# Seven block products in place of eight for four of eleven pairs of weight tiles in two down projections

## The chip, the core and the metric

The kernel runs on one core of a Trainium2 chip. The time is that of the device, in microseconds (us), of one execution; the median of several is given. TensorE (PE in the profile) multiplies, with its weight loads shown as PEld; VectorE is DVE, ScalarE is ACT, GpSimd is POOL, and the queue of weight loads is that of SyncE (SP).

## The reference

The program is one layer of each of three kinds on 256 rows of 1024 numbers in float32: a block with two feed-forward networks (FFN) around gMLP gating and stick-breaking attention, a gated linear attention with an FFN, and a block attention with an FFN. The change touches only the FFNs of the last two, each of which is followed by a layer norm:

```
def swiglu_ffn(x, w_gu, w_down):
    gate, up = jnp.split(x @ w_gu, 2, axis=-1)
    return (jax.nn.silu(gate) * up) @ w_down
```

with x of 256 x 1024, `w_down` of 2816 x 1024, and then `x = layer_norm(ALPHA * x + ffn(x))`, where ALPHA is the fourth root of 4.

## The kernel before

All products are made in three matmuls of "fp32r" type: each factor is split into a high part and a low part, and high x high, high x low and low x high are added in PSUM. Weights come in chunks of 128 x 1024 numbers (two k-tiles of 512 columns, in the down projection). A chunk goes four ways, each on another engine. SyncE's queue loads it into one of 5 slots of `raw` (`load_chunk`; the slot is free when the chunk 5 before it has been split, semaphore `wl`). ScalarE copies it, rounded, into `wh` (`high_to`, line 1000). VectorE subtracts that from `raw` into `wl` (`low_to`, line 1594); both have 9 slots. TensorE uses both and counts the chunk in `used`, which frees the slots. `lead` says how many chunks ahead of TensorE the two converting engines stand in their program order; each engine's order is written out by hand, as generators (`block`) that yield at each chunk.

An FFN has a gate and an up product in column blocks (`narrow`: nine of 256 columns, turned, so that their results already have the hidden dimension on partitions), whose product goes through HB and is split into HH and HL; and then the down projection, blocks `d0` and `d1`, one for each half of 512 output columns. Each has 22 k-tiles in 11 chunks. For each chunk TensorE makes, for both row tiles t (128 rows each), 2 k-tiles x 3 matmuls = 6 matmuls of 512 columns, so 12 in all (`pe_products`, lines 514, 521, 529). The last 5 chunks of `d1` are run first for t = 0 and then for t = 1 (`tail`), so that the layer norm of the first row tile can begin while the second is still multiplied.

VectorE adds the result of each half and row tile to `ALPHA * X` (`residual`, line 1703), takes the statistics and norms X in two passes (`layer_norm`, lines 1683 to 1698), first with `gbc`, then with `bbc`; between the two it needs the inverse root `rs`, which GpSimd computes from the variance (line 2440). `gbc` and `bbc`, the norm's gain and shift, are loaded by GpSimd's queue when the previous stage is done. In the third FFN TensorE then turns X's pieces (line 439), for the next stage: those of the first row tile before the last k-tile of the down projection, those of the second row tile in the last chunk of the next block's first row tile. In the fourth X is stored.

## Time and profile before

| what | us |
|---|---|
| median of 3 runs | 1223.21 |
| lowest and highest of them | 1222.98, 1224.38 |
| span of the profiled execution | 1221.8 |

Of one profiled execution there is a page, with busy times, the chain of work that ended last, and the costliest groups of instructions, and there are the rows of single instructions. A row gives the start, the duration, engine and line, what is written from what, and in brackets the idle time of that engine before it with what ended it. Matmuls overlap, and the end of each is a model: what one costs is read from the distance of two starts.

### The profile page before, as it was taken

The page shows a single profiled execution, that of the slowest core. Times are in us where ns is not written, and L with a number is a line of the kernel's source. Part 1 is how long each engine was busy: PE and PEld are TensorE (multiplying, and loading weights), DVE is VectorE, ACT ScalarE, POOL GpSimd, SP SyncE. Part 2 cuts the span into 40 slices and gives each one's busy share as a digit, 9 for nine tenths or more (in the row PEclk, how much of TensorE's full clock was granted, in tenths as well). Part 3 has the DMA queues.
Part 4 walks back from the last instruction along what each step waited for, and adds up shares of the span by engine and source line. Part 5 has one row for each costly group of instructions (what it writes and reads, how often), then busy time and mean ns, then how long its engine had stood idle before and what let it go on. Part 6 is the DMA issues. An engine that isn't in the chain of part 4 may idle for free.

```text
span 1221.8 us, 15988 instructions
## 1 busy us (share of the span) xinstructions
PE 1211.0 (99%) x6145; PEld 1019.5 (83%) x6145; DVE 827.1 (68%) x1190; ACT 647.3 (53%) x923; POOL 41.5 (3%) x85
## 2 busy tenths in 40 slices
PE   9999999999999999999999999999999999999997
PEld 7888888888787888888888888888888888888886
DVE  5987755756676666777547677667647777667753
ACT  7565644446666355556436554556534464556640
POOL 2000002100000000000010000000000000000000
PEclk9999999999999999999999999999999999999999
DMA  8676754754545556666647556566745444766551
GB/s 281 197 210 187 245 186 136 248 176 145 154 141 170 188 174 208 193 187 194 202 141 189 189 189 221 176 190 190 258 173 170 158 139 140 239 190 189 190 195 46
DMA packets 154747, 225.81 MB, mean 185 GB/s; under 512 B 8152, under 2 KB 85984, under 8 KB 154672
## 3 DMA queue, kind: packets, MB, share of 16 engines
q1 hardware_dynamic: 152144, 216.10, 55.7%
q0 software_dynamic: 2512, 8.69, 2.6%
q8 instruction: 49, 0.80, 0.3%
q14 instruction: 26, 0.21, 0.1%
q10 hardware_dynamic: 16, 0.00, 0.0%
HBM read 223.72 MB, written 1.05 MB: 184 GB/s over the span
## 4 chain that ended last, share of the span: by engine, by line
PE 96%; DMA 1%; DVE 1%; ACT 1%; issue 0%; SPq 0%; POOL 0%; DVEq 0%; ACTq 0%; POOLq 0%
PE ps L550 23%; PE ps L514 19%; PE ps L521 18%; PE ps L529 18%; PE ps L554 12%; PE ps L439 2%; DMA wgk<-in_gla_w_gk_dram 1%; PE ps L713 1%; PE ps L726 1%; DMA raw<-in_ff_w_gate_dram 0%; ACT wh L1000 0%; PE ps L929 0%; PE ps L696 0%; PE ps L899 0%; PE ps L655 0%
## 5 line engine op out<-in xcount | busy, mean ns | idle before, releaser
L1594 DVE TENSOR_TENSOR wl<-raw,wh 128x1024 fp32r<-128x1024 f32 x405 | 486.3, 1219 | 104.6 <-ACT wh L1000 101.8
L1000 ACT ACTIVATE wh<-raw 128x1024 fp32r<-128x1024 f32 x405 | 418.4, 1051 | 100.8 <-PE ps L529 42.1
L550 PE MATMUL ps<-XT,wh 128*128 128x512 f32 x1216 | 423.0, 392 | 0.0
L554 PE MATMUL ps<-XT,wl 128*128 128x256 f32 x1216 | 339.7, 279 | 0.0
L550 PEld LDWEIGHTS ps<-XT,wh 128*128 128x128 f32 x1216 | 227.6, 187 | 50.9
L554 PEld LDWEIGHTS ps<-XT,wl 128*128 128x128 f32 x1216 | 229.5, 189 | 0.2
L514 PE MATMUL ps<-wh,XT 128*128 128x512 f32 x510 | 203.3, 399 | 0.0
L521 PE MATMUL ps<-wl,XT 128*128 128x512 f32 x510 | 199.4, 391 | 0.2 <-DVE wl L2372 0.2
L529 PE MATMUL ps<-wh,XT 128*128 128x512 f32 x510 | 157.9, 391 | 0.0
L514 PE MATMUL ps<-wh,HHf 128*128 128x512 f32 x352 | 137.3, 390 | 0.0
L521 PE MATMUL ps<-wl,HHf 128*128 128x512 f32 x352 | 137.0, 389 | 0.0
L514 PEld LDWEIGHTS ps<-wh,XT 128*128 128x128 f32 x510 | 95.8, 188 | 21.0 <-issue 0.7
L521 PEld LDWEIGHTS ps<-wl,XT 128*128 128x128 f32 x510 | 95.9, 188 | 20.1 <-DVE wl L2372 1.3
L529 PEld LDWEIGHTS ps<-wh,XT 128*128 128x128 f32 x510 | 95.2, 188 | 19.8
L529 PE MATMUL ps<-wh,HLf 128*128 128x512 f32 x352 | 108.5, 389 | 0.0
L529 PEld LDWEIGHTS ps<-wh,HLf 128*128 128x128 f32 x352 | 66.1, 188 | 13.9
L514 PEld LDWEIGHTS ps<-wh,HHf 128*128 128x128 f32 x352 | 66.1, 188 | 13.6
L521 PEld LDWEIGHTS ps<-wl,HHf 128*128 128x128 f32 x352 | 66.1, 188 | 13.4
L1113 ACT ACTIVATE HBf<-ps 128x256 f32<-128x256 f32 x72 | 27.5, 385 | 71.9 <-PE ps L554 71.9
L1113 ACT ACTIVATE SGf<-ps 128x256 f32<-128x256 f32 x72 | 27.6, 385 | 61.3 <-PE ps L554 61.3
L1719 DVE TENSOR_TENSOR HBf<-ps,HBf 128x256 f32<-128x256 f32 x72 | 30.3, 424 | 42.0 <-ACT HBf L1113 40.3
L1719 DVE TENSOR_TENSOR SGf<-ps,SGf 128x256 f32<-128x256 f32 x72 | 30.1, 423 | 27.9 <-ACT SGf L1113 27.9
(296 smaller groups left out, 1039.9 us busy)
## 6 DMA issues: line engine op xcount, KB each, us to landing
raw<-in_ffn_w_gu_dram SPq DMA_DIRECT2D x88, 512.0 KB, 4.3
raw<-in_w_in_dram SPq DMA_DIRECT2D x56, 512.0 KB, 4.1
raw<-in_ff_w_up_dram SPq DMA_DIRECT2D x44, 512.0 KB, 4.6
raw<-in_ff_w_down_dram SPq DMA_DIRECT2D x44, 512.0 KB, 4.6
raw<-in_ffn_w_down_dram SPq DMA_DIRECT2D x44, 512.0 KB, 4.6
raw<-in_ff_w_gate_dram SPq DMA_DIRECT2D x40, 512.0 KB, 4.1
raw<-in_gla_w_in_dram SPq DMA_DIRECT2D x24, 512.0 KB, 4.6
raw<-in_moba_w_in_dram SPq DMA_DIRECT2D x24, 512.0 KB, 4.8
```

Of the source, the lines that this page charges most:

```text
L439: ins = e.transpose(ps[:, aux_bank(key), i * P:(i + 1) * P], src, ident[:, :])
L514: e.matmul(o, lh[:, kt, rows(t)], high[:, w], start=kt == 0, stop=False)
L521: e.matmul(o, lh[:, kt, rows(t)], low[:, w], start=False, stop=False)
L529: ins = e.matmul(o, ll[:, kt, rows(t)], high[:, w], start=False, stop=kt == kts - 1)
L550: e.matmul(o, wh_of(j)[:, w], XT[:, kt, :, :].rearrange("p a n -> p (a n)"), start=kt == 0, stop=False)
L554: ins = e.matmul(o[:, 0:256], wl_of(j)[:, w], XTH[:, kt, :], start=False, stop=kt == kts - 1)
L713: ins = e.matmul(o, QK[r, m, keys], QK[r, m, queries], start=True, stop=True)
L726: ins = e.matmul(y, V[:, t, 64 * h:64 * h + 64], z, start=t == 0, stop=t == 1)
L1000: e.activation(wh_of(j)[:, 0:m], raw[:, j % NR, 0:m], ACT.Copy).then_inc(S("wh"), 1)
L1113: e.activation(dst, ps[:, bank_of(name, t), 256:512], ACT.Copy).then_inc(S("part"), 1)
L1594: e.tensor_tensor(wl_of(j)[:, 0:m], raw[:, j % NR, 0:m], wh_of(j)[:, 0:m].bitcast(F32), ALU.subtract).then_inc(S("wl"), 1)
L1719: e.tensor_tensor(dst, ps[:, bank_of(name, t), 0:256], dst, ALU.add).then_inc(ev(name, t)[0], 1)
```

## The change

Take one pair of k-tiles k and k+1. Its share of the output is a product of a 2 x 2 block matrix (two row tiles by two k-tiles, of h) with another (two k-tiles by two column halves, of the weights). That takes eight block products. For four of the eleven pairs in each of the two FFNs, those of the hidden blocks `SEVEN = (1, 2, 3, 7)`, seven products of sums and differences are made in their place.

- **Sums of h.** VectorE makes four sums of 128 columns in a chain (`row_sums`), ScalarE and VectorE split them into SH and SL (`high_sums`, `low_sums`). The fourth set is split into XT at the start of the down projection.
- **Sums of the weights.** A pair has two loads, of one k-tile with all 1024 columns each, and makes four chunks: block 1 of the first tile (512 columns), the second tile, and two chunks of sums. GpSimd makes these (`weight_sums`): one difference over 1024 columns (`wsum`), then two operations over 512 columns in a chain (`wchain`). They go into SC for the first and third pair, into `gbc` and `bbc` for the second and fourth. A slot of `raw` is free when the chunk has been split and GpSimd has read it.
- **Products.** `pe_seven` makes 21 matmuls in place of 24. Three of the seven products go to PSUM banks of the block's outputs, four to banks 7, 6, 5 and 4, added up over the four pairs.
- **Putting it together.** ScalarE scales X by ALPHA during the down projection. After the last such pair, and behind the chunk conversions that `d0` has brought ahead, ScalarE copies the four banks to SBUF (`take`). GpSimd adds them to each other and to X in eight operations over 512 columns (`gather`), in front of the two inverse roots of the layer norm. VectorE adds the ordinary outputs to X. The addition for half 0 and row tile 1 now comes between the norm of the first row tile and the addition for half 1 and row tile 1.
- **Order.** The chunks of both halves are mixed in `d0` (25 chunks): two pairs with both halves, then four times four chunks of a seven-product pair and an ordinary one of half 0, then one more; `d1` keeps five. `gbc` and `bbc` are loaded for the norm when the last sum has been split.

```diff
+SEVEN_FFNS = ("f3", "f4")
+SEVEN = (1, 2, 3, 7)
...
+            def seven(s):
+                k = 2 * (SEVEN[s] + 2)
+                mixed[f].append(("seven", s, len(chunks)))
+                for kt, n in ((k, 1), (k + 1, 2)):
+                    chunks.append((wd[kt * P:(kt + 1) * P, :].rearrange("p (k n) -> p k n", k=2), n, 512, kt))
+                for _ in range(2):
+                    chunks.append((None, 2, 512, k))
...
+            products = [[(of_h(k, top), p1, first, last)],
+                        [(of_h(k + 1, top), upper[0], False, False), (of_sums(3), upper[1], False, False)],
+                        [(of_sums(0), p5, first, last), (of_sums(2), p7, first, last)],
+                        [(of_sums(1), p6, first, last), (of_h(k + 1, bottom), lower, False, False)]]
...
+                    s1, s2, s3, s4 = [SG[:, i % 2, rows(r)] for r in range(4)]
+                    own(e.tensor_tensor(s1, a21, a22, ALU.add))
+                    e.tensor_tensor(s3, a11, a21, ALU.subtract)
+                    wait_own()
+                    own(e.tensor_tensor(s2, s1, a11, ALU.subtract))
+                    wait_own()
+                    e.tensor_tensor(s4, a12, s2, ALU.subtract).then_inc(S("ssum"), 1)
...
+                        e.tensor_tensor(t13.rearrange("p (a n) -> p a n", a=2), raw[:, a:a + 2, cols(1)],
+                                        raw[:, a, :].rearrange("p (a n) -> p a n", a=2),
+                                        ALU.subtract).then_inc(S("wsum"), 1)
...
+                    own(e.tensor_tensor(t24[:, cols(0)], t13[:, cols(1)], raw[:, a, cols(0)], ALU.add))
+                    e.tensor_tensor(t24[:, cols(1)], raw[:, b, cols(0)], t24[:, cols(0)], ALU.subtract).then_inc(
+                        S("wchain"), 1)
...
+                if f in SEVEN_FFNS:
+                    kind, s, j = [item for item in mixed[f] if item[0] == "seven"][-1]
+                    e.wait_ge(S("used"), j + 4)
+                    e.wait_ge(S("hl"), len(NARROW) * (FFNS.index(f) + 1))
+                    for i, dst in enumerate((SG[:, 0, :], SG[:, 1, :], HB[:, 3, :], HB[:, 2, :])):
+                        take(i, dst)
...
+                    if f in SEVEN_FFNS:
+                        e.wait_ge(S("gathered"), 4 * SEVEN_FFNS.index(f) + 2 * t + half + 1)
+                        o = product_of(name, t)
+                        e.tensor_tensor(X[:, t, cols(half)], o, X[:, t, cols(half)], ALU.add).then_inc(
+                            ev(name, t)[0], 1)
+                        layer_norm(name, t, half, 6 if f == "f3" else 8)
...
+                e.wait_ge(S("alpha"), 2 * F + 2)
+                e.wait_ge(S("taken"), 4 * F + 2)
+                own(add(p6, p1))
+                add(X[:, 0, cols(0)], p1).then_inc(S("gathered"), 1)
+                own(add(X[:, 0, cols(1)], p6))
+                e.wait_ge(S("taken"), 4 * F + 3)
+                add(X[:, 0, cols(1)], p5).then_inc(S("gathered"), 1)
+                e.wait_ge(S("taken"), 4 * F + 4)
+                own(add(p7, p6))
+                add(X[:, 1, cols(0)], p7).then_inc(S("gathered"), 1)
+                own(add(X[:, 1, cols(1)], p7))
+                add(X[:, 1, cols(1)], p5).then_inc(S("gathered"), 1)
```

VectorE at the end of the fourth FFN's last up block and the start of its down projection, before (HLf is h's low part, wl a chunk's):

```order
L1719 TENSOR_TENSOR HBf<-ps,HBf 128x256 [waits s_part] x2
L1760 TENSOR_TENSOR HBf<-HBf,SGf 128x512 [waits s_silu,s_ev1,s_ev0]
L1594 TENSOR_TENSOR wl<-raw,wh 128x1024 [waits s_wh,s_hsum]
L1724 TENSOR_TENSOR HLf<-HBf,HHf 128x512 [waits s_hh]
L1594 TENSOR_TENSOR wl<-raw,wh 128x1024 [waits s_wh] x10
L1703 SCALAR_TENSOR_TENSOR X<-X,ps 128x512 [waits s_mm0]
```

The same place after:

```order
L1882 TENSOR_TENSOR HBf<-ps,HBf 128x256 [waits s_part] x2
L1942 TENSOR_TENSOR HBf<-HBf,SGf 128x512 [waits s_silu,s_ev1,s_ev0]
L1757 TENSOR_TENSOR wl<-raw,wh 128x512 [waits s_wh,s_hsum]
L1757 TENSOR_TENSOR wl<-raw,wh 128x1024 [waits s_wh]
L1757 TENSOR_TENSOR wl<-SC,wh 128x1024 [waits s_wh] x2
L1887 TENSOR_TENSOR HLf<-HBf,HHf 128x512 [waits s_hh]
L1904 TENSOR_TENSOR XT<-SGf,XT 128x512 [waits s_sh]
L1757 TENSOR_TENSOR wl<-raw,wh 128x1024 [waits s_wh]
L1757 TENSOR_TENSOR wl<-raw,wh 128x512 [waits s_wh]
L1757 TENSOR_TENSOR wl<-raw,wh 128x1024 [waits s_wh]
L1757 TENSOR_TENSOR wl<-gbc,wh 128x1024 [waits s_wh]
L1757 TENSOR_TENSOR wl<-bbc,wh 128x1024 [waits s_wh]
```

The splits of sums stand in the same row as those of loaded chunks, one split of h's sums has come in, and the addition to X has gone to the far side of all of them.

GpSimd in the fourth FFN, before (the roots of the previous norm, the loads, the roots of the last norm):

```order
L2440 TENSOR_TENSOR st<-st 128x1 [waits s_agg]
L2440 TENSOR_TENSOR st<-st 128x1 [waits s_agg,s_rs0]
L2421 DMA gbc<-in_ln_g_dram 128x1024 [waits s_xg11,s_rs1]
L2424 DMA bbc<-in_ln_b_dram 128x1024
L2440 TENSOR_TENSOR st<-st 128x1 [waits s_agg]
L2440 TENSOR_TENSOR st<-st 128x1 [waits s_agg,s_rs0]
```

And after, from the sums of the fourth pair on:

```order
L2652 TENSOR_TENSOR gbc<-raw 128x1024 [waits s_raw1,s_raw0,s_wl]
L2660 TENSOR_TENSOR bbc<-gbc,raw 128x512 [waits s_wsum]
L2661 TENSOR_TENSOR bbc<-raw,bbc 128x512 [waits s_pl]
L2616 DMA gbc<-in_ln_g_dram 128x1024 [waits s_wl]
L2619 DMA bbc<-in_ln_b_dram 128x1024
L2672 TENSOR_TENSOR SGf<-SGf 128x512 [waits s_taken,s_alpha]
L2672 TENSOR_TENSOR X<-X,SGf 128x512 [waits s_pl]
L2672 TENSOR_TENSOR X<-X,SGf 128x512
L2672 TENSOR_TENSOR X<-X,HBf 128x512 [waits s_taken,s_pl]
L2672 TENSOR_TENSOR HBf<-HBf,SGf 128x512 [waits s_taken]
L2672 TENSOR_TENSOR X<-X,HBf 128x512 [waits s_pl]
L2672 TENSOR_TENSOR X<-X,HBf 128x512
```

The sums and the additions stand in front of the roots, and the two loads have moved behind the last sum.

ScalarE at the end of the fourth FFN, before (conversions of the last chunks):

```order
L1000 ACTIVATE wh<-raw 128x1024 [waits s_raw4,s_used]
L1000 ACTIVATE wh<-raw 128x1024 [waits s_raw0,s_used]
L1000 ACTIVATE wh<-raw 128x1024 [waits s_raw1,s_used]
L1000 ACTIVATE wh<-raw 128x1024 [waits s_raw2,s_used]
L1000 ACTIVATE wh<-raw 128x1024 [waits s_raw3,s_used]
```

And after, with the copies out of PSUM (L1268):

```order
L1138 ACTIVATE wh<-raw 128x1024 [waits s_raw1,s_used]
L1138 ACTIVATE wh<-raw 128x1024 [waits s_raw2,s_used]
L1138 ACTIVATE wh<-raw 128x1024 [waits s_raw3,s_used]
L1268 ACTIVATE SGf<-ps 128x512 [waits s_hl,s_used]
L1268 ACTIVATE SGf<-ps 128x512
L1268 ACTIVATE HBf<-ps 128x512 x2
```

The four copies stand behind the last conversion; in the third FFN they stand behind that of the next stage's second chunk.

## Rows read from the trace of the kernel before

**Rows 1.** The page's chain that ended last, by engine.

```profile
PE 96%; DMA 1%; DVE 1%; ACT 1%; issue 0%; SPq 0%; POOL 0%; DVEq 0%; ACTq 0%; POOLq 0%
```

**Rows 2.** Busy time by stretch, both down projections: length, PE, PEld, DVE, ACT, POOL, PEclk.

```profile
862.95:922.80 59.85, 59.85 (x271) 49.62 (x269) 34.86 (x37) 24.05 (x25) 0.99 (x1) 1.00 0.57 194
1154.56:1214.45 59.89, 59.89 (x266) 49.37 (x264) 30.05 (x33) 19.56 (x20) 1.00 (x1) 1.00 0.38 133
```

**Rows 3.** Timeline of TensorE in the fourth down projection, six matmuls apart.

```profile
1165.48 0.39 PE L514 MATMUL ps<-wh,HHf 128*128 128x512 f32 x1
...
1166.84 0.39 PE L514 MATMUL ps<-wh,HHf 128*128 128x512 f32 x1
```

**Rows 4.** Groups by form: line, engine, operation, count, busy us, mean ns.

```profile
L1594 DVE TENSOR_TENSOR wl<-raw,wh 128x1024 fp32r<-128x1024 f32 x404 | 486.0, 1221 | 104.6 <-ACT wh L1000 101.8
L1000 ACT ACTIVATE wh<-raw 128x1024 fp32r<-128x1024 f32 x404 | 418.1, 1053 | 100.8 <-PE ps L529 42.1 <-DMA raw<-in_ffn_w_down_dram 21.0 <-DMA raw<-in_ff_w_down_dram 10.3
...
L1724 DVE TENSOR_TENSOR HLf<-HBf,HHf 128x512 fp32r<-128x512 f32 x36 | 24.6, 684 | 0.0
...
L1251 ACT ACTIVATE QK<-ps 128x512 f32<-128x512 f32 x8 | 4.7, 592 | 2.9 <-PE ps L439 2.9
```

**Rows 5.** Timeline of VectorE in the fourth down projection; brackets: idle before.

```profile
1158.17 5.76 DVE L1594 TENSOR_TENSOR wl<-raw,wh 128x1024 fp32r<-128x1024 f32 x5
...
1183.36 0.69 DVE L1703 SCALAR_TENSOR_TENSOR X<-X,ps 128x512 f32<-128x512 f32 x1 [9.92 <-PE ps L529]
```

**Rows 6.** Timeline of VectorE over one step of the gate and up loop.

```profile
1144.60 0.69 DVE L1760 TENSOR_TENSOR HBf<-HBf,SGf 128x512 f32<-128x512 f32 x1
...
1149.63 0.42 DVE L1719 TENSOR_TENSOR SGf<-ps,SGf 128x256 f32<-128x256 f32 x1 [0.96 <-ACT SGf L1113]
1150.58 1.23 DVE L1594 TENSOR_TENSOR wl<-raw,wh 128x1024 fp32r<-128x1024 f32 x1 [0.52 <-ACT wh L1000]
...
1153.85 0.42 DVE L1719 TENSOR_TENSOR HBf<-ps,HBf 128x256 f32<-128x256 f32 x1 [0.58 <-ACT HBf L1113]
1155.18 0.42 DVE L1719 TENSOR_TENSOR HBf<-ps,HBf 128x256 f32<-128x256 f32 x1 [0.90 <-ACT HBf L1113]
1155.69 0.69 DVE L1760 TENSOR_TENSOR HBf<-HBf,SGf 128x512 f32<-128x512 f32 x1
```

**Rows 7.** Timeline of GpSimd, two memsets.

```profile
1.74 0.20 POOL L2409 MEMSET ones<- 128x128 f32 x1
...
665.57 0.74 POOL L2507 MEMSET STm<- 128x768 f32 x1 [24.24 <-DVE KT L2225]
```

**Rows 8.** Timelines of GpSimd, and of VectorE beside it at 202.58.

```profile
197.11 0.18 POOL L2427 TENSOR_SCALAR st<-st 128x1 f32<-128x1 f32 x1
...
202.64 1.22 POOL L2427 TENSOR_SCALAR LNB<-LNB 128x2 f32<-128x2 f32 x1 [0.55 <-DVE LNB L1901]
...
202.58 1.23 DVE L1594 TENSOR_TENSOR wl<-raw,wh 128x1024 fp32r<-128x1024 f32 x1
...
628.36 0.56 POOL L2497 TENSOR_TENSOR st<-st 128x1 f32<-128x1 f32 x1 [174.68 <-DVE st L1673]
...
1209.78 1.00 POOL L2440 TENSOR_TENSOR st<-st 128x1 f32<-128x1 f32 x1 [171.70 <-DVE st L1689]
```

**Rows 9.** Timelines of VectorE and ScalarE: splits, and the conversion that waits for the reload.

```profile
1186.06 7.08 DVE L1594 TENSOR_TENSOR wl<-raw,wh 128x1024 fp32r<-128x1024 f32 x6
...
1190.81 1.06 ACT L1000 ACTIVATE wh<-raw 128x1024 fp32r<-128x1024 f32 x1 [5.03 <-DMA raw<-in_ffn_w_down_dram]
```

**Rows 10.** Timelines at the ends of the third (VectorE, TensorE) and fourth FFN (TensorE, VectorE).

```profile
927.70 1.42 DVE L1698 SCALAR_TENSOR_TENSOR X<-X,st,bbc 128x512 f32<-128x512 f32 x2
...
928.75 1.08 PE L439 MATMUL ps<-ident,X 128*128 128x128 f32 x8
...
1213.99 0.61 PE L529 MATMUL ps<-wh,HLf 128*128 128x512 f32 x2
...
1214.64 0.69 DVE L1703 SCALAR_TENSOR_TENSOR X<-X,ps 128x512 f32<-128x512 f32 x1 [2.08 <-PE ps L529]
```

210 lines of the change are left out of this document (188 added, 22 removed).

## Prediction, made before the changed kernel was run

> **What bounds the kernel now.** I read the page first: TensorE carries 96% of the chain that ended last [rows 1]. The stretches of the two down projections come next: in each TensorE is busy for every microsecond, at full granted clock [rows 2]. One chunk of twelve matmuls takes 1.36 us per six, so one matmul of 512 columns costs 0.227 us [rows 3]. Here, then, a matmul taken away is time taken away, as long as nothing else becomes late. What feeds TensorE is the pair of conversions of each weight chunk: 1.05 us on ScalarE, 1.22 us on VectorE (1.15 us apart in a row) [rows 4, 5]. VectorE is free for 9.9 us in the middle of the down projection [rows 5], so it has room today.
>
> **The saving.** A pair of k-tiles took 8 block products of 3 matmuls and takes 7: 3 matmuls fewer for each of 4 pairs in 2 FFNs, 24 x 0.227 = **5.44 us**, 2.72 us per FFN. By this alone the profiled span would go from 1221.8 to 1216.4 us.
>
> I count time in one FFN from the start of its down projection (1154.56 us in the fourth, 862.95 in the third), and number its chunks c0 to c29 (normal c0 to c3; then four times: four chunks of a seven-product pair and a normal one; c24; and c25 to c29, the last five of half 1). Of a seven-product pair the first chunk is 512 wide, the third and fourth are sums. Without a stall TensorE needs c8 at 15.6, c17 at 29.2, c22 at 36.7, c25 at 43.5, and is done with row tile 0 at 50.3 and with all at 57.1 us (before: 53.0 and 59.8).
>
> **Added work in the gate and up loops.** Per seven-product block: four VectorE operations of 128 columns in a chain with two waits (0.68 us for 512 columns and 1.22 for 1024 [rows 4] make 0.28 for 128, with the waits 1.3 us), one split of 512 columns (0.68 us), and one copy of 0.6 us on ScalarE. One step of that loop lasts 11.09 us and VectorE idles in it for 3.0 us, in waits that TensorE paces [rows 6]; 2.0 us fit in, with 1 us over. I cost it at nothing. If the cover were short, a step would start late by what is missing, but product banks have slack: the gate product is out at 1150.05 [rows 6], and its banks are needed at 1154.6.
>
> **Added work on VectorE and ScalarE in the down projection.** Four pairs turn 2 chunks of 1024 into 3.5: 6 chunks more, 6 x 1.15 = 6.9 us on VectorE and 6.3 on ScalarE. Beside 9.9 us of idle VectorE this is hidden. The two scalings of X (1.05 us each) and four copies out of PSUM (0.6 us [rows 4]) on ScalarE replace nothing but lie in idle time as well.
>
> **The weight sums on GpSimd.** Per pair one operation over 1024 columns and two over 512 that form a chain, each reading two operands. No row has such an operation. Bounds: not under VectorE's price for the same (1.2 us for 1024 [rows 4]); from above, three streams (two reads, a write) at the slope of GpSimd's memset, (0.74 - 0.20) / 640 columns = 0.84 ns a column [rows 7], 2.6 us. One read through memset's rate takes 0.9 us, so two reads alone give 1.7. I take 2.2 us for 1024 and 1.1 for 512, between two and three streams: 4.4 us per pair. The Trainium skill (GPSIMD Engine Reference, section 3, Performance versus the Vector engine) gives about 2.6 cycles an element for a two-input add, 4497 ns for 2048 columns; an estimate by it would be 2.3 us for 1024, the same sum within 0.2 us a pair, and no run here shows it yet.
>
> **The collision.** On GpSimd an operation on two elements takes 0.18 us alone, but 1.22 us when it starts 0.06 us after VectorE's 1.23 us split of a chunk, which reads two SBUF tiles; the root of one element takes 0.56 us alone, 1.00 in the fourth FFN's layer norm, where VectorE works on X and gbc [rows 8]. GpSimd is held until such an operation of VectorE is over. I take it that this works both ways: then the sums and the splits, which all read two SBUF tiles, go one after the other. That VectorE is held by GpSimd no row shows, as GpSimd never had a long operation. The Trainium skill (SBUF — State Buffer, section on the two separate sides) states it: the port pair is an exclusive lock, whoever starts first has it for the whole instruction. By that rule the sums come out as in my forecast, without it as in rival B; with the rows on GpSimd's side it agrees.
>
> The two then take turns. Work on that port from -0.5 us until c22 is split: VectorE 4 x 0.62 + 15 x 1.15 for c4 to c22, 1.2 for c3, 2.0 for the last product of h and two splits, together 22.9; GpSimd 2.2 for what is left of the first pair and 3 x 4.4 = 15.4. Sum 38.3, so c22 is ready at 37.8 at best where 36.7 is needed. The order makes it worse earlier: c8 is split at about 15, and the slot of raw that it frees holds c15 about 4.5 us later (3.6 in [rows 9], where one load stands alone), so the third pair's sums can't start before 20, their chain ends at about 26, c16 is split by 27.5, the fourth pair's first sum takes the port for 2.2 us, and c17 is split at 31 against 29.2, c18 0.8 us late on top. I take **2.0 us** of stall per FFN (0 to 5).
>
> **The tail.** ScalarE's four copies stand behind the conversion of c29 (of the next stage's second chunk, c31, in the third FFN), not behind the last seven-product pair alone. By the same turns c22 is split at 38.3 and c24 at 40.6; the load into its slot lands 3.6 us later [rows 9], conversion until 45.3, second copy at 46.5. Then GpSimd does eight additions of 1.1 us with 0.1 between, 9.6 us, and 2.2 us of waits for VectorE's splits and X operations: 58.3. Behind them on GpSimd stand the roots of both layer norms, 0.56 to 1.0 us; behind the first root VectorE has its last two X operations (1.4) and the moved residual of half 0 (0.7 + 0.7): free at 61.9. TensorE's last product would be there at 57.1 + 2.0, and is taken some 0.25 us later [rows 10], at 59.4: **2.5 us** late in the fourth FFN (0 where the copies come at 40). In the third all is 2.7 us later (two more chunks to load and convert, one more split in the way): X's first half is normed at 63.2 where TensorE turns it at 56.2 + 2.0, 5.0 us; and the moved residual (1.4 us) and the split behind it meet the split of the turned X, which today ends just in time (X is ready at 929.1, TensorE turns it from 928.75 [rows 10]): 1.0 us more, **6.0 us**. The reloads of gbc and bbc are issued behind the last sum, at about 35, and land by 41, long ahead of 52.
>
> **Sum.** -5.4 + 2 x 2.0 + 2.5 + 6.0 = +7.1 us: a span of 1228.9. The profiled run of 1221.8 lies 1.4 us under the median, so 1230.3; I say **1230.0**. I hold the ends of the unknown costs to -5 and +14.
>
> **Rivals.** A, the forecast: the port is shared by turns both ways. Range 1226 to 1236.
> B: VectorE isn't held by GpSimd's reads, or GpSimd gives way. Then splits run as today: c24 at 30, copies from 38, additions until 51, the roots in time. What stays is about 0.4 us for the moved residual in the third FFN: -5.0, 1218.2. For it speaks that no row shows VectorE held (in [rows 8] it keeps its durations); against it, that GpSimd plainly waits for VectorE on the same port.
> C: shared port but shorter sums, 1.7 us for 1024: the port's work falls by 3.5 us per FFN, the first stall vanishes, the tail shrinks to 1 us and 3: -1.4, 1221.8, inside what can't be told from no change or just outside.
> D: as A, and the stalls of 4 to 6 us let the granted clock fall to 1.2 GHz at the head of the next stage. No wait that long stands in the middle of this trace [rows 2], so nothing here prices it but the ratio of the levels: 5 us of matmuls at half speed cost 5 more: 1235 to 1242.
> E: the seven products aren't paced at 0.227 us, since each matmul has weights of its own. But each has them already in [rows 3]: little chance.
>
> **How the numbers follow.** A 0.48, B 0.27, C 0.15, D 0.07, others 0.03. About 0.2% (2.4 us) is what a measurement of this kernel tells from no change. Faster: B and a third of C, 0.33. Within: half of C and bits of A, 0.11. Slower: 0.56. The range that leaves out no more than 2 in 10 must take B in: 1217.5 to 1237. The likeliest case alone is 1226 to 1236.
>
> **What would show it.** GpSimd's subtraction over 1024 columns with a start-to-start near 2.2 us or more; splits beside it that last 2 to 3.5 us, or begin that much late, where they take 1.22 alone. TensorE waiting for wl in front of c17 and c18 of either FFN. The additions on X ending around 58, and the root behind them; X's second operation waiting for GpSimd. If splits keep 1.22 us beside the sums and the chain stays 96% TensorE, B is right and I am wrong by 12 us. If the third FFN's end shows no wait for the turned X, the tail's term fails even if the first stall is there.

## The result, and the profile after

The changed kernel takes 1238.34 us (median of 4 runs, 1237.21 to 1238.52) against 1223.45 for the kernel before: 1.0115 times as long (95% interval 1.0101 to 1.013). That is 14.9 us slower by the medians and 14.1 by the ratio. I had said 1230.0, within 1217.5 to 1237. The direction was right and the size was not: the sum said +7.1 us, the spans of the two profiled executions differ by 14.7 (1236.5 against 1221.8). One execution among all of those below, the profiled one of e13, was slow from end to end (2032.49 us, granted clock 0.556), so its time is left out and its rows aren't used.

Three anchors tell where the time lies: the third FFN's down projection starts at 862.67 us (862.95 before), the fourth's at 1165.01 (1154.56), and the last instruction ends at 1236.5 (1221.8). So 10.7 us were lost from the third down projection to the fourth, 4.2 in the fourth and behind it, and nothing ahead of either. TensorE's waits come first. Timeline of TensorE in the changed kernel, third FFN and then fourth; brackets are the idle time and what ended it:

```profile
893.22 0.50 PE L660 MATMUL ps<-wl,SHf 128*128 128x512 f32 x1 [0.89 <-DVE wl L1757]
...
895.46 0.50 PE L602 MATMUL ps<-wl,HHf 128*128 128x512 f32 x1 [0.58 <-DVE wl L1757]
...
929.60 1.97 PE L520 MATMUL ps<-ident,X 128*128 128x128 f32 x8 [8.44 <-DVE X L1861]
931.22 0.77 PE L595 MATMUL ps<-wh,HHf 128*128 128x512 f32 x1
...
939.23 1.03 PE L520 MATMUL ps<-ident,X 128*128 128x128 f32 x8
...
1193.84 0.50 PE L660 MATMUL ps<-wl,SHf 128*128 128x512 f32 x1 [0.53 <-DVE wl L1757]
...
1196.08 0.50 PE L660 MATMUL ps<-wl,SHf 128*128 128x512 f32 x1 [0.58 <-DVE wl L1757]
...
1198.31 0.50 PE L602 MATMUL ps<-wl,HHf 128*128 128x512 f32 x1 [0.58 <-DVE wl L1757]
```

There are two kinds of wait. At c17, the last chunk of the third seven-product pair, and at c18 behind it TensorE waits for low parts, in the fourth FFN at c16 as well: counted from start to start, less the 0.23 us of a matmul, 1.8 us in the third FFN and 2.2 in the fourth. (The first matmul behind each such wait takes 0.34 us to the next start, 0.11 more than the others.) And in the third FFN it waits 8.44 us for the first row tile of the turned X. The transposes behind that wait take 1.97 us where they took 1.04, and from them to the transposes of row tile 1 pass 9.63 us where 6.82 passed before (921.93 to 928.75, the latter in [rows 10]). These 2.8 us show in the granted clock, and in the starts: the matmuls of 512 columns from 931.22 to 934.35 us start 0.43 us or more apart, those from 935.57 on 0.23. Busy time by stretch (length, PE, PEld, DVE, ACT, POOL, PEclk, DMA share, GB/s):

```profile
902.00:912.00 10.00, 10.00 (x46) 8.29 (x45) 5.40 (x5) 3.57 (x4) 0.00 (x0) 1.00 0.89 330
...
922.00:932.00 10.00, 2.40 (x10) 2.30 (x11) 8.19 (x12) 0.99 (x2) 6.60 (x5) 0.66 0.18 52
932.00:942.00 10.00, 10.00 (x41) 7.98 (x41) 7.68 (x14) 4.68 (x7) 2.05 (x3) 0.83 0.31 97
```

TensorE worked without a pause, stood for 8.4 us, and came back at the lower of its two levels, 1.2 and 2.4 GHz; 0.66 and 0.83 of full speed are the means of ten microseconds each. The transposes at 1.97 us are at the lower level, those at 939.23, at 1.03 us, at the full one again.

What comes late is read off the three other engines. GpSimd, third FFN: a pair of weight sums, then the loads of the norm, then the additions and the root.

```profile
889.68 2.40 POOL L2652 TENSOR_TENSOR gbc<-raw 128x1024 f32<-128x1024 f32 x1
892.16 2.16 POOL L2660 TENSOR_TENSOR bbc<-gbc,raw 128x512 f32<-128x512 f32 x1
894.40 2.15 POOL L2661 TENSOR_TENSOR bbc<-raw,bbc 128x512 f32<-128x512 f32 x1
900.80 0.59 POOL L2616 DMA_DIRECT2D gbc<-in_ln_g_dram  x1 [4.25 <-DVE wl L1757]
...
916.06 1.30 POOL L2672 TENSOR_TENSOR SGf<-SGf 128x512 f32<-128x512 f32 x1 [14.14 <-ACT SGf L1268]
...
923.64 4.59 POOL L2672 TENSOR_TENSOR X<-X,HBf 128x512 f32<-128x512 f32 x3
928.20 0.56 POOL L2635 TENSOR_TENSOR st<-st 128x1 f32<-128x1 f32 x1
```

ScalarE beside it: the conversions of chunks c27 and c28, and the copies out of PSUM.

```profile
903.02 1.06 ACT L1138 ACTIVATE wh<-raw 128x1024 fp32r<-128x1024 f32 x1 [0.21 <-DMA raw<-in_ffn_w_down_dram]
909.41 1.06 ACT L1138 ACTIVATE wh<-raw 128x1024 fp32r<-128x1024 f32 x1 [5.33 <-DMA raw<-in_ffn_w_down_dram]
...
914.85 1.06 ACT L1268 ACTIVATE SGf<-ps 128x512 f32<-128x512 f32 x2
```

VectorE: the split of c17 and three more beside sums of GpSimd, then the norm of row tile 0.

```profile
890.91 2.26 DVE L1757 TENSOR_TENSOR wl<-SC,wh 128x1024 fp32r<-128x1024 f32 x1 [2.33 <-ACT wh L1138]
893.09 5.14 DVE L1757 TENSOR_TENSOR wl<-raw,wh 128x1024 fp32r<-128x1024 f32 x3
...
918.76 0.69 DVE L1975 TENSOR_TENSOR X<-ps,X 128x512 f32<-128x512 f32 x1 [2.56 <-POOL X L2672]
...
924.11 3.00 DVE L1855 SCALAR_TENSOR_TENSOR X<-X,st,gbc 128x512 f32<-128x512 f32 x2
928.79 1.42 DVE L1861 SCALAR_TENSOR_TENSOR X<-X,st,bbc 128x512 f32<-128x512 f32 x2 [1.68 <-POOL st L2635]
```

The split of c17 lasts 2.26 us, from 890.91 on, beside the fourth pair's first sum (889.68 to 892.08), and three splits in a row take 5.14 us where five took 5.76 in [rows 5]. L1855 takes 3.00 us for two; with no GpSimd beside it, it takes 1.40 to 1.41. The operation at 918.76 has GpSimd's additions beside it too and keeps its 0.69 us: one of its operands is in PSUM and only one in SBUF, where the held ones read two SBUF tiles. The turned X waits for L1861, that for the root, the root for the eight additions, these for the copies, the copies for the conversions of c28 to c31, and c28 for its load.

The fourth FFN ends by the same chain, without a turned X behind it. VectorE there:

```profile
1226.70 1.41 DVE L1861 SCALAR_TENSOR_TENSOR X<-X,st,bbc 128x512 f32<-128x512 f32 x2 [1.68 <-POOL st L2635]
...
1229.36 0.67 DVE L1975 TENSOR_TENSOR X<-ps,X 128x512 f32<-128x512 f32 x1
...
1232.65 1.42 DVE L1861 SCALAR_TENSOR_TENSOR X<-X,st,bbc 128x512 f32<-128x512 f32 x2
```

TensorE's last product is out at 1224.9, and VectorE takes it at 1229.36. From 1224.9 to the end pass 11.6 us, where 7.2 passed before (1214.6 to 1221.8): a tail of 4.4 us.

### The profile page after: what moved, and what is told of

Its sections match the earlier page's. It is cut to its first block and busy times, and to the rows that moved or that the text cites. A ratio compares the mean times of both kernels' runs of the same rounds, so it can differ in the third digit from the quotient of the medians.

```text
span 1236.5 us, 16140 instructions
## 1 busy us (share of the span) xinstructions
PE 1209.7 (98%) x6121; PEld 1016.0 (82%) x6121; DVE 882.0 (71%) x1246; ACT 670.6 (54%) x959; POOL 121.0 (10%) x127
## 5 line engine op out<-in xcount | busy, mean ns | idle before, releaser
L1757 DVE TENSOR_TENSOR wl<-raw,wh 128x1024 fp32r<-128x1024 f32 x405 | 495.8, 1243 | 102.5 <-ACT wh L1138 99.9
L1138 ACT ACTIVATE wh<-raw 128x1024 fp32r<-128x1024 f32 x405 | 413.9, 1042 | 83.6 <-PE ps L610 21.7
L602 PE MATMUL ps<-wl,HHf 128*128 128x512 f32 x288 | 112.6, 391 | 1.2 <-DVE wl L1757 1.2
L595 PE MATMUL ps<-wh,HHf 128*128 128x512 f32 x288 | 112.8, 392 | 0.0
L610 PE MATMUL ps<-wh,HLf 128*128 128x512 f32 x288 | 89.2, 391 | 0.0
L602 PEld LDWEIGHTS ps<-wl,HHf 128*128 128x128 f32 x288 | 54.2, 188 | 12.9 <-DVE wl L1757 2.0
L610 PEld LDWEIGHTS ps<-wh,HLf 128*128 128x128 f32 x288 | 54.3, 189 | 11.5
L595 PEld LDWEIGHTS ps<-wh,HHf 128*128 128x128 f32 x288 | 54.2, 188 | 11.1
L1175 ACT ACTIVATE XT<-ps 128x512 fp32r<-128x512 f32 x24 | 13.5, 597 | 60.7 <-PE ps L520 60.7
```

The lines of the kernel that those rows point to most:

```text
L595: e.matmul(o, lh[:, kt, rows(t)], high[:, w], start=kt == 0, stop=False)
L602: e.matmul(o, lh[:, kt, rows(t)], low[:, w], start=False, stop=False)
L610: ins = e.matmul(o, ll[:, kt, rows(t)], high[:, w], start=False, stop=kt == kts - 1)
L1138: e.activation(wh_of(j)[:, 0:m], source(j), ACT.Copy).then_inc(S("wh"), 1)
L1175: e.activation(dst, src, ACT.Copy).then_inc(high(key)[0], 1)
L1757: e.tensor_tensor(wl_of(j)[:, 0:m], source(j), wh_of(j)[:, 0:m].bitcast(F32), ALU.subtract).then_inc(S("wl"), 1)
```

## The experiments

Theory at the start: the two engines share a port of the SBUF and are held by each other, which costs the chunks' stalls; what was mis-sized is the tail, since c28 came late and with it the copies and additions. Rivals: VectorE is not held; the root is what holds; VectorE would be too full anyway. Each ratio below is to the kernel before on the same chip, with its 95% interval. That kernel's median was 1224.35 us beside e1 to e4, 1223.26 beside e5 to e8, 1223.19 beside e9 to e12 and 1224.91 beside e13 to e15; so where two kernels are compared, it is by what each stands above or below the kernel before measured beside it (the changed one 14.9 above).

**e1: the port alone.** The kernel before, with five operations of GpSimd over 1024 columns at the start of each of the two down projections:

```diff
+                    for _ in range(5):
+                        if stage == 6:
+                            own(e.memset(low, 0.0))
+                        else:
+                            own(e.tensor_tensor(low, low, high, ALU.subtract))
```

> The kernel before, with five operations of GpSimd over 128x1024 put into its idle time, beside VectorE's row of splits at the head of a down projection: in the third FFN memsets, which read nothing from SBUF; in the fourth differences of two SBUF tiles. They write a tile that nothing reads afterwards, so the output is whole. Theory (VectorE and GpSimd take turns where both read SBUF tiles): in the fourth FFN splits beside a difference last up to 3.5 us in place of 1.22 and start late, each difference takes 2.2 us alone and up to 3.4 beside a split; in the third FFN splits stay 1.15 us apart. Rival 1 (GpSimd gives way, VectorE isn't held): splits stay 1.15 us apart in both. Rival 2 (any operation of GpSimd slows VectorE): they stretch in both. The time moves by under 1 us in all cases, since splits are well ahead.

One execution, 1223.21 us, where the kernel before had 1222.81 to 1225.51. Timelines of GpSimd's memsets and of a split beside them (third FFN), then of GpSimd's differences and VectorE beside them (fourth):

```profile
861.52 5.00 POOL L2526 MEMSET SC<- 128x1024 f32 x5 [115.26 <-DVE wl L1594]
...
864.61 1.23 DVE L1594 TENSOR_TENSOR wl<-raw,wh 128x1024 fp32r<-128x1024 f32 x1
...
1153.08 14.79 POOL L2528 TENSOR_TENSOR SC<-SC 128x1024 f32<-128x1024 f32 x5 [115.27 <-DVE wl L1594]
...
1156.14 3.32 DVE L1594 TENSOR_TENSOR wl<-raw,wh 128x1024 fp32r<-128x1024 f32 x1
1159.38 2.89 DVE L1724 TENSOR_TENSOR HLf<-HBf,HHf 128x512 fp32r<-128x512 f32 x1
```

Beside differences a split takes 3.32 us in place of 1.23 and a half split 2.89 in place of 0.69: VectorE is held for 2.1 to 2.2 us, nearly a whole operation of GpSimd. It isn't beside memsets: they run from 861.52 to 866.52 us, and the split that falls among them keeps its 1.23 us. This rests on that split and two operations of 512 columns (0.69 us each, at 863.88 and 865.75), since the memsets were over when VectorE's row of splits began at 866.36. The Trainium skill (SBUF — State Buffer, section on the two separate sides) calls this port an exclusive lock; this trace agrees, in the direction that no row of before showed. Rival B has fallen.

**e2, e3, e4: sums, additions, and both, cut to one column.** Every instruction and wait stays, and nearly all of the work goes. In e2:

```diff
-                    if b == a + 1:
-                        e.tensor_tensor(t13.rearrange("p (a n) -> p a n", a=2), raw[:, a:a + 2, cols(1)],
-                                        raw[:, a, :].rearrange("p (a n) -> p a n", a=2),
-                                        ALU.subtract).then_inc(S("wsum"), 1)
...
+                    e.tensor_tensor(t13[:, 0:1], raw[:, a, 512:513], raw[:, b, 0:1], ALU.subtract).then_inc(S("wsum"), 1)
...
```

> The changed kernel with the weight sums made over one column in place of 1024 and 512, all waits kept; the weight sums are thereby left out of the computation. Theory: without long operations of GpSimd the splits run 1.15 us apart, no matmul waits for wl in either FFN (-4 us), chunks c24 to c31 are ready earlier, so the four copies come at about 40 us of the down projection in place of 52, and the eight additions are over before the roots (-14 us of tails): 1218 to 1221 us. Rival (the order of chunks, the added splits and the added waits are themselves what is late): over 1230 us still.

Measured: 1220.7 us, 0.9971 (0.996 to 0.9983), as the theory said. TensorE waits for no low part in the down projections; for the turned X it waits 1.9 us. The copies come at 43.5 us of the down projection (905.69), not quite at 40.

In e3, and with both edits in e4:

```diff
-                return e.tensor_tensor(dst, dst, src, ALU.add)
+                return e.tensor_tensor(dst[:, 0:1], dst[:, 0:1], src[:, 0:1], ALU.add)
```

> The changed kernel with the eight additions of GpSimd over one column in place of 512; most of the sum of the seven products is thereby left out. Theory: the wait for splits at c17 to c22 stays (2 us per FFN), both tails go, since the roots have nothing long in front of them: 1221 to 1224 us. Rival (tails come from late copies alone, whatever GpSimd then does): above 1230 us.

Measured: 1227.27 us, 1.0026 (1.0016 to 1.0035), 3 us over the expected band. The chunks' stalls stayed, 1.8 us in the third FFN and 1.2 in the fourth. What I had missed: without any real addition the copies still come at 915.7 us, VectorE's first operation on X waits for them, and TensorE waits 2.0 us for the turned X and then takes 8.61 us to the next turn, not 6.82.

> The changed kernel with both, the weight sums and the eight additions, over one column. Theory: all that the 24 matmuls give is there: 5.4 us less, 0.4 us given back by the moved addition in the third FFN: 1218 to 1219 us. Rival (the added work of VectorE and ScalarE, or the matmuls of other weights, cost something themselves): 1221 us or more.

Measured: 1218.27 us, 0.9951 (0.9936 to 0.9967). By the medians 6.1 us are gone, by the interval 4.0 to 7.8, which holds the 5.4. The trace is sharper. TensorE's two turns in the third FFN:

```profile
920.12 1.04 PE L520 MATMUL ps<-ident,X 128*128 128x128 f32 x8
...
926.94 1.27 PE L520 MATMUL ps<-ident,X 128*128 128x128 f32 x8
```

The down projection starts at 863.86 here, so the turns come 56.26 and 63.08 us into it, against 58.98 and 65.80 before: 2.72 us less, as forecast. From the start of the fourth (1154.74) to the end (1219.3) pass 64.56 us against 67.24, 2.68 less. So the saving is there in both, and the row sums of h, their splits, the extra chunks and copies cost nothing to be seen in them. (The span of this one execution is only 2.5 us shorter, as it started the third FFN 0.9 us later and took 2.0 us more from the second turn to the fourth down projection; why stays open.)

The parts don't add up. Taking the additions away gives 12.0 us, taking the sums away gives 18.5, both give 21.0. The sums are the larger part, and the additions cost mostly in their wake: 12.0 us with the sums in place, 2.4 without them (e2 against e4).

**e5: the norm's loads out of the weight loads' way.**

```diff
+                if stage in (6, 8):
+                    e.wait_ge(S("taken"), 4 * SEVEN_FFNS.index(f) + 1)
                 load_g(ln_g[i, k].partition_broadcast(P))
                 load_b(ln_b[i, k].partition_broadcast(P))
```

> The changed kernel, but GpSimd issues the two loads of the norm's gamma and beta tiles only after the first of the four PSUM copies (the wait stands in front of each of the two norm stages of the third and the fourth FFN), so that they no longer share the DMA engines with the weight chunks c26 to c29. Theory (the copies come about 4 us later than forecast, because ScalarE's conversions of c28 to c31, which stand ahead of the copies, wait for chunks whose loads are slowed by the norm's loads): the chunk behind ScalarE's longest DMA wait lands 2 to 4 us sooner, the copies come 2 to 4 us sooner, TensorE's wait for the turned X shrinks from 8.4 us to 5 or 6, and the time is 1232 to 1236 us. Rival (the load was late because its slot was freed late by the weight sums; the norm's loads did not matter): the same copies, within 1 us, and 1237 to 1239 us.

Measured: 1234.34 us, 1.0086 (1.0071 to 1.0101), in the theory's band. The wait for the turned X is 6.94 us, where the theory had 5 or 6. ScalarE of e5, the conversion of c28 and the copies:

```profile
906.33 1.06 ACT L1138 ACTIVATE wh<-raw 128x1024 fp32r<-128x1024 f32 x1 [2.56 <-DMA raw<-in_ffn_w_down_dram]
...
911.69 1.07 ACT L1268 ACTIVATE SGf<-ps 128x512 f32<-128x512 f32 x2
```

Two loads of 512 KB that I had costed at nothing delay c28 and the copies by 3.1 us on the trace's axis, by 2.5 counted from the start of the down projection (862.10 here, 862.67 in the changed kernel), and the end by 3.8. From the split that frees its slot to its conversion c28 takes 5.3 us here and 7.8 in the changed kernel. GpSimd's first addition comes only 2.1 us sooner (913.97 against 916.06), since the two loads now stand in front of it.

**e6: the copies ahead of the conversion of c28.**

```diff
+                        if j == seventh + 9:
...
+                            e.wait_ge(S("used"), seventh + 4)
+                            e.wait_ge(S("hl"), len(NARROW) * (FFNS.index(f) + 1))
+                            for i, dst in enumerate((SG[:, 0, :], SG[:, 1, :], HB[:, 3, :], HB[:, 2, :])):
+                                e.activation(dst, ps[:, SEVEN_BANKS[i], :], ACT.Copy).then_inc(S("taken"), 1)
...
                     e.wait_ge(*source_ready(j))
                     e.activation(wh_of(j)[:, 0:m], source(j), ACT.Copy).then_inc(S("wh"), 1)
```

> The changed kernel with ScalarE's four PSUM copies placed ahead of its conversion of the fourth weight chunk from the end, right behind the last seven-product chunk that TensorE has used, in place of behind all conversions. Theory (the late copies are the mis-sized term): the copies come some 10 us sooner, GpSimd's eight adds begin and end as much sooner and no longer hold up the sums of the norm in the third FFN; there TensorE's wait for the turned X falls under 3 us and the clock stays up; the stalls of 2 us per FFN at the seven-product chunks stay: 1227 to 1231 us. Rival (the eight adds collide with VectorE's last conversions instead and move the wait into the chunks of half 1): TensorE waits for the low parts of the last chunks, 3 to 6 us per FFN in place of the tail, and the time is 1233 to 1238 us.

Measured: 1229.43 us, 1.0048 (1.0033 to 1.0063), in the theory's band. It gives 8.7 us for moving four copies. But TensorE still waits 3.55 us for the turned X, where the theory said under 3, and loses 1.9 us by the clock behind it. VectorE of e6:

```profile
911.30 8.81 DVE L1759 TENSOR_TENSOR wl<-raw,wh 128x1024 fp32r<-128x1024 f32 x4 [5.34 <-ACT wh L1146]
920.04 0.68 DVE L1977 TENSOR_TENSOR X<-ps,X 128x512 f32<-128x512 f32 x1
```

The early additions run beside the last splits: four take 8.81 us, where they take 5.09 in e9. So in part the rival's collision happened too: TensorE waits for low parts at 913.48 and 915.71, 1.8 us from start to start, and the rest lands in the wait for the turned X.

**e7: the root of row tile 0 between the fourth and the fifth addition.**

```diff
                 add(X[:, 0, cols(1)], p5).then_inc(S("gathered"), 1)
+                root(stage, 0)
                 e.wait_ge(S("taken"), 4 * F + 4)
...
```

> The changed kernel with GpSimd's root of row tile 0 placed between its fourth and its fifth add in the third and fourth FFN, in place of behind all eight. Row tile 0 has all of its columns after the fourth add. Theory (the root of tile 0 waits behind the adds of tile 1, and TensorE waits for that root): TensorE's wait for the turned X in the third FFN falls from 8.4 us to 3 to 5 us, the granted clock there stays above 0.9, which gives back up to 2.8 us more; in the fourth FFN little: 1230 to 1234 us. Rival (the clock falls after the shorter wait as well, or tile 1 becomes the late one): 1234 to 1237 us.

Measured: 1237.27 us, 1.0111 (1.0094 to 1.0128): a miss, 3 us above the theory's band and at the upper end of the rival's. Timelines of GpSimd and of VectorE in e7:

```profile
925.59 1.00 POOL L2634 TENSOR_TENSOR st<-st 128x1 f32<-128x1 f32 x1 [2.92 <-DVE st L1852]
...
926.96 3.21 DVE L1861 SCALAR_TENSOR_TENSOR X<-X,st,bbc 128x512 f32<-128x512 f32 x2
```

The root comes 2.6 us sooner (925.59 against 928.20). But GpSimd now idles 2.9 us for the statistics, and the additions of tile 1, pushed back, hold L1861 (3.21 us for two, 1.42 alone). The wait falls to 6.19 + 0.56 us, a new wait of 0.7 us for a low part comes in at 913.47, and the next turn of TensorE starts at 939.08, against 939.23. The time is 0.9 us lower, and the two intervals overlap. Moving the root alone trades one hold for another; this doesn't show that its place costs nothing once the additions are out of the way.

**e8: everything on VectorE**, sums ahead of the split of each pair's first chunk, additions ahead of its first operation on X, copies early.

```diff
+                    if j in group_of and group_of[j][1] == 0:
+                        sums_of_weights(j)
                     e.wait_ge(S("wh"), j + 1)
...
                 if f in SEVEN_FFNS:
+                    gather(f)
                     down(0, 0)
```

> The seven-product scheme whole, nothing of it on GpSimd: the weight sums are made on VectorE, in front of its split of the first chunk of each seven-product pair, the eight adds on VectorE in front of its last add of the down projection's half 1 for row tile 0, and ScalarE's four copies stand early. VectorE's added work is 4 pairs by about 3.7 us per FFN (1.24 us per 1024 columns of a two-input operation, 0.7 per 512) and eight adds of about 0.7 us, beside splits that no longer wait for the other engine. Theory (the price of the change is the sharing of the SBUF port between the two engines and where the adds stand, not the amount of work): the stalls at the seven-product chunks vanish or stay under 1 us per FFN and the tails come back to those of the kernel before plus at most 1 us: 1218 to 1221 us, faster than both. Rival (VectorE is too full for it: 71 per cent of the span, more in the down projection): TensorE waits for low parts by 3 us or more per FFN, 1224 to 1230 us.

Measured: 1226.34 us, 1.0027 (1.0017 to 1.0036). The number lies in the rival's band, but neither expectation names what happened. The waits for low parts are gone, so VectorE is not too full for the sums. But TensorE waits 4.60 us for the turned X in the third FFN, because VectorE first waits 5.6 us for the chunk that is late, makes its last four splits, and only then, from 912.18 to 917.5, adds.

**e9: as e8, the additions in that idle time**, ahead of the split of c28.

```diff
+                    for f in SEVEN_FFNS:
+                        if j == [item for item in mixed[f] if item[0] == "seven"][-1][2] + 9:
+                            gather(f)
...
                     e.wait_ge(S("wh"), j + 1)
```

> As the all-on-VectorE kernel, but the eight adds stand ahead of VectorE's split of the fourth weight chunk from the end, where VectorE was seen to wait 5.6 us for a chunk, in place of behind the splits, where they stood in front of the sums of the norm (third FFN: adds from 912.2 to 917.5, and TensorE then waited 4.6 us for the turned X). Theory (the amount of added VectorE work is free as long as it lies in VectorE's own idle time, and 4.6 us of wait and the clock that it costs go): no wait for the turned X beyond 2 us in the third FFN, fourth FFN's down projection starts near 1155, 1218 to 1220.5 us, faster than both kernels. Rival (the splits behind the adds come later and TensorE waits for them in the last chunks): a wait for low parts of 2 us or more per FFN, 1222 to 1226 us.

Measured: 1219.30 us, 0.997 (0.9958 to 0.9981), 3.9 us faster than the kernel before and 19 faster than the changed one, as the theory said. Timelines of VectorE and TensorE in e9:

```profile
896.57 4.63 DVE L1813 TENSOR_TENSOR wl<-raw,wh 128x1024 fp32r<-128x1024 f32 x4
902.00 0.69 DVE L1761 TENSOR_TENSOR SGf<-SGf 128x512 f32<-128x512 f32 x1 [0.81 <-ACT SGf L1142]
...
905.39 2.02 DVE L1761 TENSOR_TENSOR X<-X,HBf 128x512 f32<-128x512 f32 x3
907.53 5.09 DVE L1813 TENSOR_TENSOR wl<-raw,wh 128x1024 fp32r<-128x1024 f32 x4
...
919.10 1.32 PE L520 MATMUL ps<-ident,X 128*128 128x128 f32 x8 [0.19 <-DVE X L1917]
...
922.81 0.73 PE L610 MATMUL ps<-wh,XT 128*128 128x512 f32 x2 [0.56 <-DVE XT L1856]
...
927.38 1.32 PE L520 MATMUL ps<-ident,X 128*128 128x128 f32 x8 [0.19 <-DVE X L1917]
```

The eight additions fill 902.0 to 907.4. No wait for low parts is left, and the granted clock stays at 1.00 through both turns. From the first turn to the second pass 8.28 us all the same, 1.46 more than before: the transposes start later one by one (1.32 us for eight), TensorE waits 0.56 us for XT, and again a little at the second turn; so of the saving of 5.4 us some 1.8 are still lost here. VectorE is busy for 72% of the span, 71% in the changed kernel: the work is the same, GpSimd's 79 us are gone, and VectorE's busy time did not rise, since it is no longer held.

**e10: as e9, with the sums back on GpSimd.** The edit undoes the first part of e8's, the call of `sums_of_weights`.

> The same place of the eight adds on VectorE and the early copies, but the weight sums stay on GpSimd as in the changed kernel. Theory (stalls at the seven-product chunks come from the two engines' turns at the SBUF port, 2.0 us per FFN, and add to the rest): 1222 to 1224.5 us, with TensorE's waits at the chunks as in the changed kernel (1.3 and 1.0 us). Rival (these waits are swallowed by later slack): within 1 us of the kernel with everything on VectorE.

Measured: 1226.24 us, 1.0024 (1.0014 to 1.0034), 6.9 us over e9 where I had expected some 4. Of these, 5.3 are stalls for low parts (start to start, with the slower matmul behind each): 2.0 in the third FFN and 2.5 in the fourth, as in the changed kernel, and 0.8 at 913.11, among the last chunks, which I had not named. The rest comes by the late slots: the row of five splits that starts at 895.43 in e9 starts at 900.25 here, the copies come at 904.31 against 900.81, and TensorE waits 1.64 us for the turned X, with 8.67 us from turn to turn. So a part of "late copies" is the sums themselves.

**e11: the changed kernel with the sums on VectorE**, the additions and late copies left.

> The changed kernel with the weight sums on VectorE and the eight adds and the late copies left as they are. Theory (4.0 us of stalls at the chunks go; the late copies stay, as their cause is a DMA wait): 1232 to 1235 us, TensorE waits for no low part in the chunks, wait for the turned X in the third FFN 6 to 9 us. Rival (the slots of the weight ring are now freed sooner, the chunks land sooner and the copies too): copies 2 us or more sooner than 914.85, wait for the turned X under 6 us, 1228 to 1232 us.

Measured: 1229.38 us, 1.0054 (1.004 to 1.0068): in the rival's band. ScalarE of e11:

```profile
905.88 1.06 ACT L1138 ACTIVATE wh<-raw 128x1024 fp32r<-128x1024 f32 x1 [7.31 <-DMA raw<-in_ffn_w_down_dram]
...
910.78 1.07 ACT L1268 ACTIVATE SGf<-ps 128x512 f32<-128x512 f32 x2
```

c28 and the copies come 3.5 and 4.1 us sooner than in the changed kernel (2.8 and 3.3 counted from the start of the down projection, 861.94 here): the sums on GpSimd freed the weight ring's slots late. The row of splits that frees them starts at 894.88, 5.6 us sooner, so the load gave part of that back: the norm's two loads (895.54) now stand right in front of c28's, which is converted 9.8 us after its slot is free. The wait for the turned X is still 7.17 us, though, where the rival said under 6: TensorE, with no stalls left, is sooner there as well.

**e12: early copies and late norm loads together**, all of the arithmetic still on GpSimd.

> Both repairs of the load path together, everything still on GpSimd: early copies, and the norm's loads issued behind the first copy. Theory (the early copies already bring the adds out of the norm's way; what is left of the tail is VectorE's last four splits, held up by the adds, 8.8 us for four against 4.9): the norm's loads no longer slow the last chunks, so these splits begin 1 to 3 us sooner, 1226 to 1229 us. Rival (the loads do not matter once the copies are early): 1229 to 1230 us, as with the early copies alone; and if the norm's loads now come too late for the norm, over 1231 us with VectorE waiting for gbc or bbc.

Measured: 1227.72 us, 1.0037 (1.0023 to 1.0051), 1.6 us under e6; the two intervals overlap, so the times alone don't tell them apart. The last splits do start 3.6 us sooner than in e6 (907.69 against 911.30). Moving things alone repairs 10.4 of the 14.9 us.

**e13, e14, e15: a wait and nothing else.** The kernel before, with VectorE taking a statistic 4, 8 or 12 times more in the third FFN's norm:

```diff
                 own(e.bn_stats(bn[:, t, half, :], X[:, t, cols(half)]))
...
+                if stage == 6 and t == 0:
+                    for _ in range(8):
+                        wait_own()
+                        own(e.bn_stats(bn[:, t, half, :], X[:, t, cols(half)]))
```

> The kernel before, with VectorE taking the statistics of row tile 0's second half four more times in the third FFN's norm (about 0.73 us each, 2.9 us in all). The turn of X had about 1 us in hand. Theory (a short wait costs itself and no clock): TensorE waits some 2 us, the clock of the stretch behind stays above 0.9, and the time rises by 1.5 to 2.5 us. Rival (any wait of 2 us brings the clock down): rises by 3.5 us or more.

> The same with eight more (about 5.8 us in all). Theory (a wait of 4 to 5 us is followed by products at half clock, which cost 1 to 3 us more): TensorE waits 4.5 to 5 us, the granted clock of the 10 us around it falls to 0.7 to 0.9, the time rises by 6 to 8 us. Rival (the half clock in the changed kernel had another cause): the clock stays and the time rises by 4.5 to 5 us.

> The same with twelve more (about 8.8 us in all), near the 8.4 us that TensorE waits in the changed kernel. Theory: TensorE waits some 7.8 us and loses 2.5 to 3 us more to the clock, as in the changed kernel: 10 to 11 us above the kernel before. Rival (no clock cost): 7.5 to 8 us.

Measured: e13 1.0009 (1.0 to 1.0019), 1.1 us with an interval of 0 to 2.3; that leaves no room for a wait of 2 us and a loss by the clock of 2 us beside it. From e14 to e15 four more statistics lengthen the wait by 2.91 us; by an estimate from these two, the wait in e13 was 4.08 - 2.91, some 1.2 us, which is all of its time. e14 1.0049 (1.0033 to 1.0065), 6.0 us by the ratio and 5.7 by the medians; e15 1.0068 (1.0051 to 1.0085), 8.3 and 7.9. TensorE of e14, then of e15:

```profile
925.89 1.97 PE L439 MATMUL ps<-ident,X 128*128 128x128 f32 x8 [4.08 <-DVE X L1702]
...
935.39 1.03 PE L439 MATMUL ps<-ident,X 128*128 128x128 f32 x8
```

```profile
928.63 1.97 PE L439 MATMUL ps<-ident,X 128*128 128x128 f32 x8 [6.99 <-DVE X L1702]
...
937.53 1.03 PE L439 MATMUL ps<-ident,X 128*128 128x128 f32 x8
```

The clock cost is real and needs no seven products. From turn to turn pass 9.50 and 8.90 us in place of 6.82: 2.7 us lost behind a wait of 4.1, 2.1 behind one of 7.0. By its time alone e15 would fit the rival without a clock cost (7.5 to 8); the rows decide, since its wait was 6.99 us and not the 7.8 of the forecast, the granted clock of 922 to 932 us is 0.70 (0.66 in e14), and its second turn comes 8.8 us later than before, as much as its span is longer. I had let the loss grow with the wait, and it does not. Turn to turn, less 6.82, in the other kernels:

| kernel | wait for the turned X, us | lost behind it, us |
|---|---|---|
| e10 | 1.64 | 1.85 |
| e3 | 2.05 | 1.8 |
| e6 | 3.55 | 1.9 |
| e14 | 4.08 | 2.7 |
| e8 | 4.60 | 2.6 |
| e5 | 6.94 | 1.7 |
| e15 | 6.99 | 2.1 |
| changed | 8.44 | 2.8 |
| e12 | 2.88 | 1.5 |
| e11 | 7.17 | 1.5 |
| e7 | 6.19 + 0.56 | 3.1 (less the 0.56) |

In all of these the matmuls behind the wait stand 0.43 us apart for a stretch, and later 0.23. In e2 and e9 none does and the clock stays at 1.00, and yet 1.46 us are lost from turn to turn, in small waits; so a loss by this measure is the clock's only where the starts show it. What sets a wait's loss within 1.5 to 3.1 us stays open, and so does where the loss begins: e2 waits 1.91 us and its clock stays up, and e13 shows none, while e10 loses 1.85 us behind a wait of 1.64.

## Why the prediction was wrong in its size, point by point

| term, us | forecast | measured | from |
|---|---|---|---|
| fewer products | -5.4 | -5.4 | e4's anchors |
| stalls at the chunks | 2 x 2.0 | 1.8 and 2.2 | TensorE's waits |
| third FFN: wait for the turned X | 5.0 + 1.0 | 8.4 | TensorE's wait |
| third FFN: clock | none | 2.8 | turn to turn |
| fourth FFN's tail | 2.5 | 4.4 | end less last product |
| rest | 0 | 0.5 | difference; all but 0.1 found, see the end |
| sum | 7.1 | 14.7 | spans |

**The saving** was right; e4's trace shows it with all but the sums' and additions' columns in place. So was **added work in the gate and up loops** at nothing, as far as can be seen: the third down projection starts 0.3 us sooner than before, and over all traces here at 861.94 to 863.86 us. Rival E, pacing, has fallen with them.

**The weight sums.** I took 2.2 us for 1024 columns and 1.1 for 512. In the trace the least are 2.40 and 1.28, where GpSimd is hardly held; beside VectorE's splits the six rows of 1024 columns go up to 3.22, and most sums of 512 columns show 1.62 to 2.17. With that rival C, shorter sums, has fallen. The estimate by the Trainium skill (GPSIMD Engine Reference, section 3, Performance versus the Vector engine) was 2.3 us for 1024, and the trace's least, 2.40, agrees within 5%.

**The collision** went as written, by turns, and is confirmed by e1. The 2.0 us per FFN are well hit, 1.8 and 2.2, and not by luck: TensorE waits in front of c17 and c18, the two named, because the fourth pair's first sum comes in between; in the fourth FFN it waits at c16 too. And the rule of the lock held against rival B, by which the change would have gained.

**The tail** is the step that failed, and in it "the load into its slot lands 3.6 us later". c24 was split at 40.1 us of the third FFN (902.8), where I had 40.6; but the load into its slot, c29's, is converted from 911.36 on, 8.6 us later, so that the conversion ends at 49.7 in place of 45.3. From the second copy to the last addition pass 12.3 us, where I had 11.8, with some luck, as one addition takes 1.28 to 1.30 us and not 1.1, and the waits were shorter. Three things lie in it. First, "the reloads of gbc and bbc are issued behind the last sum, at about 35, and land by 41, long ahead of 52". I asked whether they are late for their own reader and not whom they make late. They are issued at 38, as c26 to c29 load, and c28 takes 7.8 us from the split that frees its slot (c23's, the first of five from 900.43 on, over at 901.6) to its conversion, where I had 3.6 from a load that stood alone. e5 prices this: 2.5 of these 7.8 us, 2.6 on the copies, 3.8 on the time; the 1.7 us that c28 still takes over 3.6 stay open. The DMA share alone would not have shown it: it is 0.89 from 902 to 912, and 0.96 in the same stretch of the kernel before. Second, the second copy was to come at 46.5 in the fourth FFN and 49.2 in the third; it came at 49.7 and 53.2. In the third this is 4 us, and the wait for the turned X is 3.4 us longer than the 5.0 forecast. e11 shows that the sums, by way of late slots, hold the copies up by 3.3 us of the FFN's own time. The late slots I had in the sum (c24 at 40.6), but with the short load behind them. Third, the 1.0 us for the moved residual meeting the turned X is not seen as a wait.

**The clock** was a rival with 0.07, and it should have been a term. Rival D said "stalls of 4 to 6 us let the granted clock fall", priced at as much again as the stall. The forecast itself had a stall of 5 us there, so the case was not beside the forecast but inside it. The price was too high: 2.8 us are lost behind 8.4. e14 and e15 show that such a wait costs 2 to 3 us more in this very place, whatever causes it. With 2.8 us for the clock the sum would have been +9.9, 1233.

**"Behind them on GpSimd stand the roots"** was true as an order; e7, which moved the root and gained 0.9 us, doesn't price it alone, since the additions behind the root then held VectorE.

**The range** reached to 1237 and the time was 1238.3: the late load and the clock came together, and rival D, the one case above 1237, had 0.07.

The rest of 0.5 us is found but for 0.1: the slower matmul behind each chunk's stall (0.2 and 0.3 us), and 0.2 that the wait for the turned X is longer from start to start (8.60), less the 0.3 by which the third FFN starts sooner. What stays open: what else slows c28's load, and where the clock's loss begins.

## What to carry to other kernels

Before giving arithmetic to GpSimd because it is idle, ask how many SBUF operands its operations and those of VectorE beside it read: a wide two-operand operation of the one holds the other for nearly its whole length, and here the same sums cost 6.9 us less on an engine that is 72% busy either way. Where a step hands on to a chain, put it where the engine already waits: moving four copies gave 8.7 us, eight additions 7.0. Ask of each moved load whom it delays, not only whether it is early enough; and expect a wait of 3 us or more of a TensorE that had been busy to cost more than its length, here by 1.5 to 3.1 us.
